# Prompt attention of a hybrid decoder layer: heads of two branches take turns, one PSUM bank per group, sums from the exponentials

## The reference

```python
H_A = 8; KV_A = 2; H_B = 8; HEAD_DIM = 64; SEQ = 512

def sparse_gqa(q, k_sel, v_sel, valid):          # branch A: keys chosen by an indexer, 2 kv heads for 8 heads
    qg = q.reshape(B, Q, KV_A, H_A // KV_A, HEAD_DIM)
    logits = jnp.einsum('bqgrd,bqkgd->bqgrk', qg, k_sel).astype(jnp.float32) * HEAD_DIM ** -0.5
    logits = jnp.where(valid[:, :, None, None, :], logits, -jnp.inf)
    p = jax.nn.softmax(logits, axis=-1).astype(v_sel.dtype)
    o = jnp.einsum('bqgrk,bqkgd->bqgrd', p, v_sel)
    return o.reshape(B, Q, H_A * HEAD_DIM)

    # branch B (moba_prompt, block_attend): causal attention over blocks of 256 keys; with two blocks in
    # the prompt, a query sees its own block up to itself and the whole block before it
    p = jax.nn.softmax(jnp.concatenate([s_sel, s_own], axis=-1), axis=-1).astype(v_own.dtype)
    o = (jnp.einsum('bqhk,bkhd->bqhd', p[..., n_flat:], v_own)
         + jnp.einsum('bqhnk,bqhnkd->bqhd', p_sel, v_sel))
```

## Time and profile before

| | |
|---|---|
| median of 3 runs | 1198.89 us (1191.41 to 1204.62) |
| the profiled execution | 1191.15 us; span of its instructions 1189.3 us |
| mean granted TensorE clock | 0.906 of full speed |
| TensorE, VectorE, ScalarE, GpSimd busy | 83%, 35%, 23%, 13% of the span |
| DMA | 246.56 MB, mean 207 GB/s |

### The profile page before, as it was taken

The page is one execution under the profiler, slowest core; times in us unless marked ns, Lnnn a source line. Parts: engine busy times, 40 slices in busy tenths (PEclk is TensorE's granted clock), DMA queues, the critical chain, the costliest instruction groups (busy, mean ns, idle before and its releaser), DMA issues. The chain is left out here.

```text
span 1189.3 us, 14006 instructions
## 1 busy us (share of the span) xinstructions
PE 981.8 (83%) x5685; PEld 577.0 (49%) x5685; DVE 420.8 (35%) x912; ACT 272.6 (23%) x436; POOL 155.2 (13%) x183
## 2 busy tenths in 40 slices
PE   6999999887989999775799999999459686877850
PEld 5544444566765665221579999644223222222220
DVE  3213888544337595122053322022441101111016
ACT  4122221454335677310100000011201000000002
POOL 1100000121012334333300000000011110101110
PEclk9999999999579999887889999999669888988895
DMA  7212201123245997999655450380539999999946
GB/s 265 84 71 80 91 10 36 56 63 98 71 149 214 348 337 242 401 388 408 219 126 178 133 170 19 107 304 36 172 99 366 375 368 361 368 356 371 367 158 225
DMA packets 140783, 246.56 MB, mean 207 GB/s; under 512 B 15136, under 2 KB 106640, under 8 KB 132400
## 3 DMA queue, kind: packets, MB, share of 16 engines
q1 hardware_dynamic: 118688, 142.39, 36.0%
q0 software_dynamic: 21408, 101.05, 23.1%
q10 hardware_dynamic: 624, 2.23, 0.5%
HBM read 238.26 MB, written 15.77 MB: 214 GB/s over the span
## 5 line engine op out<-in xcount | busy, mean ns | idle before, releaser
L686 PE MATMUL bank<-ring,hT 128*128 128x512 f32 (+1 forms) x384 | 161.0, 574 | 0.0
L686 PEld LDWEIGHTS bank<-ring,hT 128*128 128x128 f32 x384 | 72.0, 192 | 79.4 <-issue 70.4
L1047 PEld LDWEIGHTS bank<-consts,ring 128*128 128x128 f32 x704 | 79.0, 144 | 40.7 <-ACT kT_s L1263 33.4
L1263 ACT COPY kT_s<-bank 128x1024 f32<-128x1024 f32 (+1 forms) x90 | 85.7, 997 | 51.9 <-PE bank L1047 51.8
L1047 PE MATMUL bank<-consts,ring 128*128 128x128 f32 x704 | 90.9, 283 | 3.1 <-PEq L229 1.6
L2129 DVE TENSOR_TENSOR sgm<-sgm,bank 128x256 f32<-128x256 f32 x16 | 6.7, 422 | 221.1 <-ACT sgm L1985 221.1
L1939 PE MATMUL bank<-early,obT 128*64 128x512 f32 x352 | 79.0, 602 | 2.4 <-DVE obT L2124 1.4
L1660 PE MATMUL bank<-w_o,uT 128*128 128x512 f32 (+1 forms) x160 | 69.5, 593 | 2.6 <-PEq L242 2.6
L1534 PE MATMUL bank<-hT_hi,gate_w_hi 128*128 128x272 f32 x224 | 65.9, 294 | 0.0
L1534 PE MATMUL bank<-hT_hi,gate_w_lo 128*128 128x272 f32 x224 | 64.6, 288 | 0.0
L1534 PE MATMUL bank<-hT_lo,gate_w_hi 128*128 128x272 f32 x224 | 64.5, 288 | 0.0
(11 more groups left out here) (352 smaller groups left out, 1463.0 us busy)
## 6 DMA issues: line engine op xcount, KB each, us to landing
early<-in_w_e_gate SPq DMA_DIRECT2D x22, 1024.0 KB, 13.2
early<-in_w_e_up SPq DMA_DIRECT2D x22, 1024.0 KB, 13.2
early<-in_w_e_down SPq DMA_DIRECT2D x16, 1024.0 KB, 12.7
uT<-in_w_e_down SPq DMA_DIRECT2D x16, 1024.0 KB, 11.9
ring<-in_w_in SPq DMA_DIRECT2D x5, 2048.0 KB, 8.4
w_o<-in_w_e_gate SPq DMA_DIRECT2D x10, 1024.0 KB, 12.6
w_o<-in_w_e_up SPq DMA_DIRECT2D x10, 1024.0 KB, 12.9
gate_w<-in_w_in SPq DMA_DIRECT2D x14, 512.0 KB, 5.2
```

The lines of the kernel that those rows point to most:

```text
L686: last = nc.tensor.matmul(bank[:, n % 4, 0:WID[g]], s.hT[:, k, t * P:(t + 1) * P], w[:, gi % 2, k, 0:WID[g]], start=(k == 0), stop=(k == K ...
L1047: last = nc.tensor.transpose(bank[:, u, e * P:(e + 1) * P], ring[:, slot, at:at + P], ident)
L1263: nc.scalar.copy(kT[:, n % 2, u, :], bank[:, u, :]).then_inc(kT_kept, 1)
```

## The change

Three things are changed, all of them around `prompt`.

The order: ITEMS now takes the two groups of a tile together, pair by pair, so b and a items alternate. A list ENDS holds the number of each group's last item, and the places of `normalise`, `turn_out` and `keep_out`, and the waits for them, follow from it.

The banks: `weigh` puts both heads of a group into one bank, 6 for b and 7 for a, since two groups are now open at once; a group's first product waits for the scaling of the group before the last. The turned outputs go to bank 4 or 5.

The sums: `exps` has ScalarE accumulate each exponential's sum over its row (accum_out) into `sums`; V loses its column of ones (`vbP`, `vaP`, 64 columns), the two memsets go, and `normalise` takes the reciprocal of `sums` before it waits for the products.

```diff
     GROUPS = [(kind, t) for t in (3, 2, 1, 0) for kind in "ba"]
-    ITEMS = [(g, kind, t, j) for g, (kind, t) in enumerate(GROUPS) for j in range(PAIRS)]
+    ITEMS = [(2 * i + q, *GROUPS[2 * i + q], j) for i in range(len(GROUPS) // 2) for j in range(PAIRS) for q in range(2)]
+    ENDS = [max(m for m, item in enumerate(ITEMS) if item[0] == g) for g in range(len(GROUPS))]
...
-        inv = sb("inv", [P, 2, PAIRS])
+        sums, inv = sb("sums", [P, 4, 2, PAIRS]), sb("inv", [P, 2, 2, PAIRS])
...
+        def ended(m):
+
+            return sum(end + 3 <= m for end in ENDS)
...
             def turn(m):
-                g, _, t, j = ITEMS[m]
+                t = ITEMS[m][2]
                 pe.wait_ge(exp_done, 2 * (m + 1))
                 if m >= 1:
                     pe.wait_ge(tr_kept, m)
-                if g >= 1:
-                    pe.wait_ge(oT_kept, g - 1 if j < 2 else g)
+                if ended(m):
+                    pe.wait_ge(oT_kept, ended(m))
...
             def weigh(m):
                 g, kind, t, j = ITEMS[m]
                 pe.wait_ge(tr_kept, m + 1)
-                if j == 0 and g >= 1:
-                    pe.wait_ge(on_ready, g)
+                if j == 0 and g >= 2:
+                    pe.wait_ge(on_ready, g - 1)
                 for half in range(2):
                     for c in range(t + 1):
-                        v = s.va1[:, c, half, :] if kind == "a" else s.vb1[:, c, 2 * j + half, :]
-                        last = nc.tensor.matmul(bank[:, 6 + half, j * (HD + 1):(j + 1) * (HD + 1)],
+                        v = s.vaP[:, c, half, :] if kind == "a" else s.vbP[:, c, 2 * j + half, :]
+                        at = (half * PAIRS + j) * HD
+                        last = nc.tensor.matmul(bank[:, 6 + g % 2, at:at + HD],
                                                 probT[:, m % 2, half, c * P:(c + 1) * P], v,
                                                 start=(c == 0), stop=(c == t))
...
             def turn_out(g):
                 pe.wait_ge(on_ready, g + 1)
-                pe.wait_ge(tr_kept, min(PAIRS * (g + 1) + 2, n))
+                pe.wait_ge(tr_kept, min(ENDS[g] + 3, n))
                 for j in range(PAIRS):
-                    last = nc.tensor.transpose(bank[:, 4, j * P:(j + 1) * P], on[:, g % 2, j * P:(j + 1) * P], ident)
+                    last = nc.tensor.transpose(bank[:, 4 + g % 2, j * P:(j + 1) * P], on[:, g % 2, j * P:(j + 1) * P], ident)
...
                     nc.scalar.activation(prob[:, m % 3, half, 0:width(t)], bank[:, 2 * (m % 2) + half, 0:width(t)],
-                                         ACT.Exp, bias=ntop[:, m % 4, half:half + 1]).then_inc(exp_done, 1)
+                                         ACT.Exp, bias=ntop[:, m % 4, half:half + 1],
+                                         accum_out=sums[:, g % 4, half, j:j + 1]).then_inc(exp_done, 1)
...
             def normalise(g):
                 kind, t = GROUPS[g]
-                dve.wait_ge(weighed, PAIRS * (g + 1))
+                dve.wait_ge(exp_done, 2 * (ENDS[g] + 1))
                 if g >= 2:
                     dve.wait_ge(oT_done, g - 1)
-                o = bank[:, 6:8, 0:PAIRS * (HD + 1)].rearrange("p a (j d) -> p a j d", d=HD + 1)
-                link(nc.vector.reciprocal(inv[:, :, :], o[:, :, :, HD]))
-                nc.vector.tensor_tensor(on[:, g % 2, :].rearrange("p (j a d) -> p a j d", a=2, d=HD), o[:, :, :, 0:HD],
-                                        inv[:, :, :].unsqueeze(3).to_broadcast([P, 2, PAIRS, HD]), ALU.mult)\
+                link(nc.vector.reciprocal(inv[:, g % 2, :, :], sums[:, g % 4, :, :]))
+                dve.wait_ge(weighed, ENDS[g] + 1)
+                o = bank[:, 6 + g % 2, :].rearrange("p (a j d) -> p a j d", a=2, d=HD)
+                nc.vector.tensor_tensor(on[:, g % 2, :].rearrange("p (j a d) -> p a j d", a=2, d=HD), o,
+                                        inv[:, g % 2, :, :].unsqueeze(3).to_broadcast([P, 2, PAIRS, HD]), ALU.mult)\
                     .then_inc(on_ready, 1)
```

More of the change, by code:

```diff
@@ L224, in build @@
                         s.kbT = sq("kbT", [P, PAIRS, SEQ])
-                        s.vb1 = sq("vb1", [P, TP, H, HD + 1])
-                        s.va1 = sq("va1", [P, TP, 2, HD + 1])
+                        s.vbP = sq("vbP", [P, TP, H, HD])
+                        s.vaP = sq("vaP", [P, TP, 2, HD])
                         s.score = sq("score", [P, TP, SEQ])
@@ L335, in project @@
         idx_done, relu_done, acc_done = sem("pj_idx_done"), sem("pj_relu_done"), sem("pj_acc_done")
-        v1_ready = sem("pj_v1_ready")
         chain_v = sem("pj_vector_chain")
@@ L386, in _ @@
                     sp.dma_start(o["v_b_p"][t * P:(t + 1) * P, :].rearrange("t (h d) -> t h d", d=HD),
-                                 s.vb1[:, t, :, 0:HD]).then_inc(vb_stored, 16)
+                                 s.vbP[:, t, :, :]).then_inc(vb_stored, 16)
                 else:
@@ L397, in _ @@
             nc.gpsimd.memset(s.ones[:, :], 1.0)
-            nc.gpsimd.memset(s.vb1[:, :, :, HD:HD + 1], 1.0)
-            nc.gpsimd.memset(s.va1[:, :, :, HD:HD + 1], 1.0)
             for n, (g, t) in enumerate(ITEMS):
@@ L474, in keep_projected @@
                 if g == "vb" and t < TP:
-                    nc.scalar.copy(s.vb1[:, t, :, 0:HD], src.rearrange("p (h d) -> p h d", d=HD)).then_inc(nat_ready, 1)
+                    nc.scalar.copy(s.vbP[:, t, :, :], src.rearrange("p (h d) -> p h d", d=HD)).then_inc(nat_ready, 1)
                     return
@@ L566, in prompt_rows @@
                     return
-                link(nc.vector.tensor_copy(s.va1[:, t, :, 0:HD], b[:, KVW:2 * KVW].rearrange("p (a d) -> p a d", d=HD)))
+                link(nc.vector.tensor_copy(s.vaP[:, t, :, :], b[:, KVW:2 * KVW].rearrange("p (a d) -> p a d", d=HD)))
                 link(nc.vector.tensor_scalar(s.wi[:, t, :], b[:, KI0 + HD:KI0 + HD + H], IDX_SCALE, None, ALU.mult))
@@ L841, in _ @@
                     weigh(m - 2)
-                if m >= PAIRS + 2 and (m - 2) % PAIRS == 0:
-                    turn_out((m - 2) // PAIRS - 1)
+                if m - 3 in ENDS:
+                    turn_out(ENDS.index(m - 3))
         @block.scalar
@@ L847, in exps @@
             def exps(m):
-                _, _, t, _ = ITEMS[m]
+                g, _, t, j = ITEMS[m]
                 for half in range(2):
@@ L866, in keep_out @@
                 nc.scalar.copy((s.oaT if kind == "a" else s.obT)[:, :, t * P:(t + 1) * P],
-                               bank[:, 4, :].rearrange("p (j r) -> p j r", j=PAIRS)).then_inc(oT_kept, 1)
+                               bank[:, 4 + g % 2, :].rearrange("p (j r) -> p j r", j=PAIRS)).then_inc(oT_kept, 1)
             for m in range(n + 3):
@@ L873, in _ @@
                     keep_turned(m - 1)
-                if m >= PAIRS + 2 and (m - 2) % PAIRS == 0:
-                    keep_out((m - 2) // PAIRS - 1)
+                if m - 3 in ENDS:
+                    keep_out(ENDS.index(m - 3))
         @block.vector
@@ L908, in _ @@
                     tops(m)
-                if m >= PAIRS + 1 and (m - 1) % PAIRS == 0:
-                    normalise((m - 1) // PAIRS - 1)
+                if m - 2 in ENDS:
+                    normalise(ENDS.index(m - 2))
 def sample(nc, s, a):
```

## The result

The changed kernel takes 1205.05 us (median of 20 runs, 1198.69 to 1211.86 apart from one disturbed run of 1486.61, which is left out of the ratio), the kernel before, run beside it on the same chip, 1199.66 us (20 runs, 1187.98 to 1205.48). The ratio is 1.0051, with a 95% interval of 1.0028 to 1.0075: half a per cent slower. The forecast of 1204 us held. Its composition did not, as the rows show.

The account below looks back on a forecast made before the run. It took a loop through TensorE, VectorE and ScalarE to bound the prompt attention. Order -0.5 us plus reads +5.6 gave +5.1, taking the median from 1198.89 to 1204 us, range 1193 to 1212.

Parts of the forecast that it names:

- The loop: Prompt attention: TensorE, VectorE and ScalarE wait on each other in a cycle; 8.70 us per two a-head items in tile 3.
- the serial steps: At group ends the next scores wait a whole chain, up to 6.57 us; seven become six, in pairs near 254, 284, 311.
- the link: On ScalarE the copy of turned probabilities stands behind the next exponentials, and TensorE's next turning needs that copy.
- The order: Alternating a and b items in the prompt attention: -0.5 us, give or take 2.
- the added "+1": Items 9 to 25, tiles 2 and 1: taken as 57 us after the change, against 55.97 before, including half-clock stretches.
- the 0.8: Start of tile 3: the first b pairs now run at the a heads' slower pace, costing +0.8 us.
- The reads: ScalarE's accumulator reads behind the 64 exponentials: 0.14 us each for 40 that count, +5.6 us (3.6 to 7.6).
- 20 visits: Times an item's two reads count: two serial steps and three loops per tile, 40 reads; the other 24 are hidden.
- The bank per group and 64 columns: Products with V never sat idle, so a second bank and one column fewer were forecast to gain 0.
- The lower clock: Rival: paired serial steps bring TensorE's half clock before about 285 us, slowing tile 1; +8 us, 1212; 12%.
- the forecast's own sign of being wrong: In the changed profile, the fall of TensorE's granted clock moving away from 298 us would show the forecast wrong.
- The sum: Whole kernel: order -0.5 plus reads +5.6 gives +5.1 us, for a median of 1204 us.

Follow-up runs that it names:

- e4: Kernel before with ScalarE's copy of the turned probabilities moved ahead of the next item's exponentials: 1173.69 us, ratio 0.9807.
- e1: Changed kernel without accum_out in the exponentials (sums a constant one), keeping new order, banks and 64 columns: 1191.53 us, ratio 0.997.
- e7: Changed kernel with one extra, unused matmul ahead of each of the first six sets of output transposes: 1196.29 us, ratio 1.0015.
- e2: Kernel before with accum_out added to the exponentials, sums written but unused: 1201.93 us, ratio 1.0047.
- e9: Changed kernel with accum_out on the a heads' exponentials only, b's sums a constant one: 1196.34 us, one run.
- e10: Changed kernel with accum_out on the b heads' exponentials only, a's sums a constant one: 1201.04 us, one run.
- e3: Changed kernel with items in the old order (all of b, then all of a), the rest kept: 1198.61 us, ratio 1.0016.
- e5: Changed kernel again without an edit, for its clock and spread: 1202.24 us, ratio 1.0059.
- e11: Kernel before with the next item's scores issued ahead of each set of output transposes: 1197.01 us, ratio 0.9997.
- e8: Changed kernel with the second output transposes of tiles 3, 2 and 1 and their copies two items later: 1199.39 us, ratio 1.0032.

## Why the prediction was right, point by point

**The loop and the serial steps: shown.** The a heads' loop is 8.74 us without reads (forecast the 8.70 of before), items 4 to 9 take 22.41 (forecast 22.3), the first two pairs of serial steps came near 255 and 286 us (forecast 254 and 284), the third at 317 and 321, at half clock, where 311 was forecast, and e4 removes the link and with it 23 us of the stage, of which some 8 by the clock.

**The order, forecast -0.5 us, "give or take 2": 0 to -3 at an equal clock.** In e1 tile 3 gave -1.6, where the forecast had -1.7. Items 9 to 17 took 31.22 us, equal to the 31.11 before, where the forecast had one or two microseconds more for items 9 to 25; e7, at full clock and with reads, did 17 to 25 in 24.05 against 24.86. The step that failed is the added "+1" for tiles 2 and 1, of which the stretch at half clock was most. The start cost more than the 0.8: e1 lost 1.4 there, with the clock at half once more from 217 to 220 us, where before it was full from 214.

**The reads, forecast +5.6 us at 0.14 each: mis-sized.** A read costs its successor 0.09 to 0.10, which was the lower bound of the estimate; the middle was taken without a row for it. Of the forecast's 20 visits with two reads each, 40 x 0.095 makes 3.8 us; e2 measures +3.4 at an equal clock, and the changed kernel less e1 +3.7 to +5.3. That 20 visits count and the rest don't is borne out by e9 and e10 for the loops, and in the old order by e2 for the serial step in tile 2 (+0.18); for the paired steps of the new order the runs don't show it apart.

**The bank per group and 64 columns, forecast 0: right.** The products with V idle 0.0 us before and after, and e3 against e2 shows no difference. The rule of the Trainium skill (Perfetto Trace Analysis, Optimizing Tensor Performance, Matmuls) had nothing to win here, as no product waited for a bank.

**The lower clock, a rival at 12%: in part what happened.** The forecast said that the clock's fall would stay at 298 us. It came at 286 in the profile, so the forecast's own sign of being wrong, a fall that moves away from 298, was there. That is the rival's place to within a microsecond or two (it asked for a fall ahead of about 285), and it cost 7.2 us in the items that the rival named, for which it had 8. In e5 it came at 282 and lifted again, in e7 not before 303, and in e11, in the old order and without reads, at about 275. So it was wrong to take it as one case beside others, there or not: it is a share of the time, different in each run, and by the fit the changed kernel draws some 5 us of it on average beside e5, perhaps 4 in the first comparison. The step that failed is the one that took the clock of one profiled execution as the kernel's own; the profile of before, at 1191.15 us and 0.906, was one of its faster runs (median 1199.66). The Trainium skill (TensorE: Matmul & The Clock Gate, A second HAM failure mode) tells of a bf16 kernel in which short idle times between groups of matmuls make the clock swing; the runs here agree in that work put into such idle times (e7) raised the mean clock from 0.894 to 0.908.

**The sum was right partly by offset.** Reads 3.8 instead of 5.6 and the order up to 2 us lower than forecast leave +1 to +3; the clock brought it back to the +5 to +7 measured. That 1204 was met so closely is luck. The reading that the change makes no difference of 1% stands on the loop, and that was right for its reason: none of its parts touches the copy's place.

**Open.** Neither the reads in the old order (e2 0.899, e3 0.901) nor the new order without reads (e1 0.900) lowered the mean clock; only both together did (0.893, 0.894). Which of their combined waits does it, and whether the pairing of the serial steps is needed, the runs don't tell: e8, which parts them, had 0.898, and e9 kept the clock full through such a pair. Why the piece between the stage and the merge scatters by 6 us among the profiles (its granted clock at 550 to 650 us was 0.83 in the changed kernel's and 0.90 before) is open too.

## What to carry to other kernels

When a loop through several engines sets the pace, look for the instruction in it that stands in its engine's order behind a wait that it doesn't need, and move that one: here two exchanged lines on ScalarE gave 2%, while reordering items, adding a bank and dropping columns around the same loop gave nothing that shows in the median. Price an added instruction by the distance to its successor's start, not by its duration, and only where the engine is not idle in front of it anyway. And before you sum against one profiled execution, see where its clock stands among the runs; an effect that goes through the clock is a share in every run, not a case that either comes or doesn't.

## What the runs showed of the hardware

An accumulator read lasts 0.19 to 0.20 us and delays the next ScalarE instruction by 0.09 to 0.10, with 128 to 512 columns alike in its own length (64 reads, mean 196 ns). Most of the scatter of this kernel's times goes with the mean granted clock, some 7.4 us per 0.01. Most of it arises ahead of the merge's table load: the two profiles of the changed kernel stand 8.95 us apart there (612.79 and 603.84) and 6.8 at their end, while the 179 us behind it, up to the read at 791.55, were within 0.5 us the same in all thirteen profiles. And more work can be faster: twelve more TensorE instructions in the stage's waits went with 8 to 17 us less of TensorE's busy time there (95.96 against 103.53 and 113.08 in two profiles without them) and a median 6 us lower.
